# A two-block transformer kernel: the merged attention in another order over its units, and two splits moved

## What is computed

```python
# layer 0, eight heads each, four blocks of 128 queries, causal
logits = einsum(q, k) * 96**-0.5;  p = softmax(where(k_idx <= q_idx, logits, -1e30));  o1 = p @ v
z = einsum(q, k) * 64**-0.5                          # stick breaking
mask = k_idx < q_idx
log_1m_beta = where(mask, log_sigmoid(-z), 0)
suffix = cumsum(log_1m_beta, reverse) - log_1m_beta
o2 = where(mask, exp(log_sigmoid(z) + suffix), 0) @ v
# mixer of the second block
qk = silu(causal_depthwise_conv(xn @ w_in[:, :2048], conv_w, conv_b))      # width 4
# each expert, on its block of 128 rows
hb = silu(xb @ w1[e]) * (xb @ w3[e]);  out = hb @ w2[e]
```

## Time and profile before

| | |
|---|---|
| median of 3 runs (lowest to highest) | 2888.7 us (2888.36 to 2888.79) |
| the profiled execution | 2887.3 us |
| its span, first to last instruction | 2885.6 us |
| mean granted TensorE clock | 0.939 |
| merged attention | about 142 to 320 us |
| mixer's projection | about 1448 to 1604 us |
| expert loop | about 2240 to 2830 us |

### The profile page before, as it was taken

The page is one execution under the profiler, slowest core; times in us unless marked ns, Lnnn a source line. Parts: engine busy times, 40 slices in busy tenths (PEclk is TensorE's granted clock), DMA queues, the critical chain, the costliest instruction groups (busy, mean ns, idle before and its releaser), DMA issues. The chain is left out here.

```text
span 2885.6 us, 30599 instructions
## 1 busy us (share of the span) xinstructions
PE 2657.8 (92%) x12110; PEld 2158.0 (75%) x12110; DVE 1522.2 (53%) x2085; ACT 1234.1 (43%) x1570; POOL 122.6 (4%) x166
## 2 busy tenths in 40 slices
PE   6998999999998999999989969798995899999994
PEld 5866778888887777888877658677874777877774
DVE  4555444344323654434466443245346788888884
ACT  3366432223334742213222222324242677777773
POOL 0111000000140000000000000000002000000001
PEclk9967799999998999999989989899997899999997
DMA  3300132433431023342322022221304899999993
GB/s 130 119 1 1 50 120 93 139 109 119 138 110 37 1 76 116 108 146 88 117 88 88 30 95 88 73 88 59 142 14 190 345 392 396 395 396 396 396 392 119
DMA packets 157146, 432.84 MB, mean 150 GB/s; under 512 B 11051, under 2 KB 80838, under 8 KB 144582
## 3 DMA queue, kind: packets, MB, share of 16 engines
q1 hardware_dynamic: 148950, 400.90, 38.1%
q10 hardware_dynamic: 4608, 16.78, 1.4%
q0 software_dynamic: 3440, 13.11, 1.3%
HBM read 383.58 MB, written 47.19 MB: 149 GB/s over the span
## 5 line engine op out<-in xcount | busy, mean ns | idle before, releaser
L307 PE MATMUL ps<-area,area 128*128 128x512 f32 (+1 forms) x1696 | 658.5, 388 | 0.0
L330 DVE TENSOR_TENSOR area<-area,area 128x2048 fp32r<-128x2048 f32 (+4 forms) x161 | 340.5, 2117 | 598.5 <-ACT area L324 598.5
L306 PE MATMUL ps<-area,area 128*128 128x512 f32 (+5 forms) x1432 | 552.0, 385 | 0.0
L324 ACT ACTIVATE area<-area 128x2048 fp32r<-128x2048 f32 (+4 forms) x161 | 284.1, 1767 | 615.6 <-PE ps L307 582.4
L2324 DVE TENSOR_TENSOR area<-area,area 128x2048 fp32r<-128x2048 f32 x192 | 433.9, 2286 | 107.3 <-ACT area L2319 107.3
L305 PE MATMUL ps<-actT_parts,area 128*128 128x512 f32 x968 | 385.4, 398 | 11.6 <-DVE area L330 9.4
L306 PE MATMUL ps<-actT_parts,area 128*128 128x512 f32 x968 | 383.3, 396 | 0.0
L2319 ACT ACTIVATE area<-area 128x2048 fp32r<-128x2048 f32 x192 | 361.0, 1913 | 48.5 <-PE ps L2353 18.4
L307 PEld LDWEIGHTS ps<-area,area 128*128 128x128 f32 x1696 | 320.4, 189 | 68.3
L306 PEld LDWEIGHTS ps<-area,area 128*128 128x128 f32 x1432 | 277.5, 194 | 52.8
L305 PE MATMUL ps<-area,actT_parts 128*128 128x512 f32 (+3 forms) x704 | 274.6, 390 | 39.6 <-DVE area L330 30.8
(11 more groups left out here) (329 smaller groups left out, 3205.3 us busy)
## 6 DMA issues: line engine op xcount, KB each, us to landing
area<-in_w SPq DMA_DIRECT2D x96, 2048.0 KB, 10.1
area<-in_w_in SPq DMA_DIRECT2D x16, 2048.0 KB, 7.9
area<-in_l_w_gate SPq DMA_DIRECT2D x22, 1024.0 KB, 5.4
area<-in_l_w_up SPq DMA_DIRECT2D x22, 1024.0 KB, 8.0
expert_inputs<-maskz SPq DMA_DIRECT2D x39, 512.0 KB, 8.7
area<-in_l_w_in SPq DMA_DIRECT2D x9, 2048.0 KB, 8.2
area<-expert_inputs SPq DMA_DIRECT2D x32, 512.0 KB, 9.7
expert_rows<-area ACTq DMA_DIRECT2D x32, 512.0 KB, 8.6
```

Source lines behind the costliest of these rows:

```text
L306: pe.matmul(dst(r), a.l, b.h, start=False, stop=False)
L307: m = pe.matmul(dst(r), a.h, b.l, start=False, stop=end)
L324: eng.activation(w.h, raw, ACT.Copy).then_inc(w_hi, 1)
L330: dve.tensor_tensor(w.l, raw, w.high_f, ALU.subtract).then_inc(w_lo, 1)
```

## The change

```diff
-                            score_banks=(0, 1), turn_banks=(2,), value_banks=(6,), prep_bank=2)
+                            score_banks=(0,), turn_banks=(2,), value_banks=(6,), prep_bank=2)
...
             def sb_bank(v):
-                return ps[:, 3 + v % 2, 0:causal(v)]
+                return ps[:, (1, 3, 4)[v % 3], 0:causal(v)]
...
             def two_pe(pe, ch):
-                for v in range(U0 + 4):
-                    sb_pe(pe, v)
-                    mla.pe(pe, v)
+                for v in range(U0 + 5):
+                    sb_scores(pe, v)
+                    mla.pe_preps(pe, v)
+                    mla.pe_scores(pe, v)
+                    sb_turn(pe, v - 4)
+                    mla.pe_values(pe, v - 3)
+                    mla.pe_turn(pe, v - 2, v)
+                    sb_values(pe, v - 5)
 
             def two_act(act, ch):
                 act.preload_act_table_set("natural_log_exp_and_others")
-                for v in range(U0 + 3):
-                    sb_act(act, ch, v)
-                    mla.act(act, v)
+                for v in range(U0 + 4):
+                    mla.act_copy(act, v - 3)
+                    if v:
+                        mla.act_exp(act, v - 1)
+                    t1 = T1[:, v % 4, 0:causal(v)]
+                    if v < U0:
+                        act.wait_ge(b_sc, v + 1)
+                        if v >= 4:
+                            act.wait_ge(b_w, v - 3)
+                        ch.mark(act.activation(t1, sb_bank(v), ACT.Abs))
+                    taken = ch.n
+                    mla.act_preps(act, v)
+                    if v < U0:
+                        ch.wait(taken)
+                        ch(act.activation(t1, t1, ACT.Exp, scale=-1.0))
+                        act.activation(t1, t1, ACT.Ln, bias=1.0).then_inc(b_t1, 1)
+                    sb_weights(act, v - 3)
+                    sb_copy(act, v - 4)
 
             def two_dve(dve, ch):
-                for v in range(U0 + 5):
-                    sb_dve(dve, ch, v)
-                    mla.dve(dve, ch, v)
+                for v in range(U0 + 6):
+                    sb_logs(dve, v - 1)
+                    mla.dve_out(dve, ch, v - 4)
+                    sb_out(dve, v - 6)
+                    sb_scan(dve, ch, v - 1)
+                    sb_less(dve, ch, v - 1, ch.n)
+                    mla.dve(dve, ch, v)
```

**Mixer's projection**, on ScalarE and on VectorE alike:

```diff
-                    if c % 4 == 3:
+                    if c % 4 == 1:
                         msp.after(act, at_qk[j])
```

**Experts**, on VectorE:

```diff
                         if q == p:
                             gated(dve, n)
-                        if q == p + 2:
+                        if q == p + 1:
                             turned_low(dve, n)
```

More of the change, by code:

```diff
@@ L870, in pe, with pe_preps @@
             def pe(self, pe, v):
-                units, nsc, npt = self.units, len(self.sc_banks), len(self.pt_banks)
+                self.pe_preps(pe, v)
+                self.pe_scores(pe, v)
+                self.pe_turn(pe, v - 2, v)
+                self.pe_values(pe, v - 3)
+            def pe_preps(self, pe, v):
                 for n, (at, _, blocks, _, _) in enumerate(self.preps):
@@ L880, in pe, with pe_scores @@
                         m.then_inc(s_pr, 1)
-                if self.mlstm and v < units and v % NT == 0:
+            def pe_scores(self, pe, v):
+                nsc = len(self.sc_banks)
+                if self.mlstm and v < self.units and v % NT == 0:
                     if v:
@@ L884, in pe @@
                     self.exponents(pe, v // NT).then_inc(s_pr, 1)
-                if v < units:
+                if v < self.units:
                     if v >= nsc:
@@ L888, in pe, with pe_turn @@
                     self.scores(pe, v, self.bank(v), self.pre0).then_inc(s_sc, 1)
[L889 to L890 removed]
+            def pe_turn(self, pe, u, v):
+                npt = len(self.pt_banks)
+                if 0 <= u < self.units:
                     pe.wait_ge(s_ex, self.ex0 + u + 1)
@@ L899, in pe, with pe_values @@
                     m.then_inc(s_pt, 1)
-                if 3 <= v < units + 3:
-                    u = v - 3
+            def pe_values(self, pe, u):
+                if 0 <= u < self.units:
                     pe.wait_ge(s_pe, self.pe0 + u + 1)
@@ L911, in act, with act_preps @@
             def act(self, act, v):
-                units = self.units
+                self.act_preps(act, v)
+                self.act_copy(act, v - 2)
+                self.act_exp(act, v)
+            def act_preps(self, act, v):
                 for n, (at, done, _, d, gain) in enumerate(self.preps):
@@ L925, in act, with act_exp @@
                     act.activation(self.PT[:, u % 2, 0:L], self.turned(u, 0, L), ACT.Copy).then_inc(s_pe, 1)
-                if v < units:
+            def act_exp(self, act, v):
+                if v < self.units:
                     L = self.length(v)
@@ L943, in act, with dve_out @@
                                        accum_out=col(rs, v)).then_inc(s_ex, 1)
[L945 to L949, removed]
+            def dve_out(self, dve, ch, u):
+                if 0 <= u < self.units:
                     h, i = divmod(u, NT)
@@ L954, in dve @@
                     dve.tensor_scalar(self.dst(h, i), self.value_at(u), col(rinv, u), None, ALU.mult).then_inc(s_on, 1)
-                    last = False
+            def dve(self, dve, ch, v):
+                units, mlstm, length = self.units, self.mlstm, self.length
+                last = 4 <= v < units + 4 and len(self.vb) > 1
                 if v < units:
@@ L1470, in sb_pe, with sb_weights @@
                     m.then_inc(b_o, 1)
[L1472 to L1482, removed]
+            def sb_weights(act, u):
+                if 0 <= u < U0:
                     act.wait_ge(b_m2, u + 1)
@@ L1492, in sb_act, with sb_scan, sb_less, sb_logs @@
                     act.activation(PT2[:, u % 2, 0:L], ps[:, 5, 0:L], ACT.Copy).then_inc(b_pe, 1)
-            def sb_dve(dve, ch, v):
-                if 5 <= v < U0 + 5:
-                    u = v - 5
+            def sb_scan(dve, ch, u):
+                if 0 <= u < U0:
+                    L = causal(u)
+                    dve.wait_ge(b_m1, u + 1)
+                    if u >= 4:
+                        dve.wait_ge(b_pt, u - 3)
+                    ch.mark(dve.tensor_tensor_scan(Pb2[:, u % 4, 0:L][:, ::-1], ones[:, 0:1].to_broadcast([P, L]),
+                                                   T1[:, u % 4, 0:L][:, ::-1], 0.0, ALU.mult, ALU.add))
+            def sb_less(dve, ch, u, scanned):
+                if 0 <= u < U0:
+                    p = Pb2[:, u % 4, 0:causal(u)]
+                    ch.wait(scanned)
+                    dve.tensor_tensor(p, sb_bank(u), p, ALU.subtract).then_inc(b_w, 1)
+            def sb_logs(dve, u):
+                if 0 <= u < U0:
+                    dve.wait_ge(b_t1, u + 1)
+                    t1 = T1[:, u % 4, 0:causal(u)]
+                    dve.scalar_tensor_tensor(out=t1, in0=sb_bank(u), scalar=0.0, in1=t1,
+                                             op0=ALU.max, op1=ALU.add).then_inc(b_sp, 1)
+            def sb_out(dve, u):
+                if 0 <= u < U0:
                     h, i = divmod(u, NT)
@@ L1512, in sb_dve, with drop_sums @@
[L1512 to L1516, removed]
+            def drop_sums(po, u):
+                if 0 <= u < U0:
+                    dg = T1[:, u % 4, causal(u) - P:causal(u)]
+                    po.wait_ge(b_sp, u + 1)
+                    po.affine_select(out=dg, in_=dg, compare_op=ALU.is_gt, fill=0.0,
+                                     base=0, pattern=[[-1, P]], channel_multiplier=1).then_inc(b_m1, 1)
@@ L1518, in two_po, with drop_weights @@
+            def drop_weights(po, u):
+                if 0 <= u < U0:
+                    dg = Pb2[:, u % 4, causal(u) - P:causal(u)]
+                    po.wait_ge(b_w, u + 1)
+                    po.affine_select(out=dg, in_=dg, compare_op=ALU.is_gt, fill=NEG,
+                                     base=0, pattern=[[-1, P]], channel_multiplier=1).then_inc(b_m2, 1)
             def two_po(po, ch):
                 for v in range(U0 + 1):
[L1520 to L1530, removed]
-            def two_pe(pe, ch):
-                for v in range(U0 + 4):
-                    sb_pe(pe, v)
-                    mla.pe(pe, v)
+                    drop_sums(po, v)
```

32 lines of the change are left out of this document (11 added, 21 removed).

## The result

The changed kernel takes **2813.6 us** (median of four runs, 2811.63 to 2813.82) against 2888.5 for the kernel before, a ratio of 0.9742 with a 95% interval of 0.9728 to 0.9756. The forecast was 2833, faster, with a range of 2808 to 2874: the side and the range held, and 75 us were gained where 56 were forecast. The profiled execution took 2813.81 us with a span of 2812.0.

What follows compares the result with a forecast made beforehand. A loop through ScalarE, VectorE and TensorE was taken to set the merged attention's pace, with TensorE's work inflated by the low clock. Merged attention -33, mixer -9, experts -14: 2887.3 - 56 + 1.4 = 2832.7 us, range 2808 to 2874.

Steps and rivals of the forecast that it cites:

- point (a): Merged attention: VectorE's logarithm step belongs to the unit before, so the value product waits for a logarithm finished an iteration ago.
- point (c): Merged attention: the stick-breaking score comes first in TensorE's iteration, so ScalarE's three activations run during five other TensorE steps.
- The low clock of the second head: Merged attention: one head at the low clock, 25.0 us, and 5 us given back for one more clock drop.
- The later heads: Merged attention: six heads at the high clock, 14.8 us each, 88.8 us together.
- The drain: End of the merged attention: 9 us for the last units, against 14 before.
- The bound of -49: Merged attention: best case, seven heads at the high clock, 103.6 us, plus 9 us of drain.
- The single bank: Merged attention: one softmax score bank makes a loop of some 3.1 us, hidden under 3.45; one wait, some 0.9 us a head.
- (b): Merged attention: the transposes come a unit later, so their exponentials are done and TensorE need not wait.
- Rival 4: Expert loop: the edit does nothing because the transfers bind; -42 in all, 2847 us; chance 0.12.
- The first, the clock up at once: Merged attention: sustained activity releases the throttle from the first full head; -72 in all, 2817 us; chance 0.14.
- The second: Merged attention: the single softmax bank binds, 0.6 us more a unit; -40 in all, 2849 us; chance 0.16.
- The third: Merged attention: the clock stays low, 25.0 us a head, stage 28 us longer; +5 in all, 2894 us; chance 0.08.

Runs made afterwards that it cites:

- the filling: The changed kernel with idle identity transposes in the first units' stops, 12 more ahead of unit 4's softmax score than in the shorter filling: 2803.7 us.
- the shorter filling: The changed kernel with 32 idle identity transposes: 8 and 6 behind the first two preparations, 6 ahead of the softmax score in units 1 to 3: 2810.9 us.

## Why the prediction was right, and where it was short

**What bounds it.** Right in the main. The loop over L1515, L954 and L907 costs what the prediction says, through its waits and through the clock: with the logarithm put back the stage took 231.6 us. That it would come out slower than the old kernel had not been foreseen. Which share of the 48.7 us the lag of the logarithm, point (a), brings alone, and which the early score, point (c), was not tested.

**Merged attention, -33 forecast, -48.7 measured.** The mechanism held, three sizes were off.

- *The low clock of the second head* ("one head at the low clock (25.0) ... I give back 5 for one more drop of the clock"). The head took 19.0 us, as the clock rose in its midst at 172 us: 6 us. The clock did not fall again: 5 us.
- *The later heads*, 14.0 us and not 14.8: 4 us over five heads. The 13.8 for TensorE's work at the high clock was too much: it is busy for 13.2 us a head (65.82 over five), so the low clock's 25.0 should have been divided by 1.9 and not by 1.81. The wait of 0.76 us stands where 0.9 was put.
- *The drain*, 0.7 us.

Together 15.7. The bound of -49 has the measured value by luck: it puts the second head at 14.8 instead of 19.0, 4.2 us too few, and the five later ones 4 us too many. The reason for the give-back was that I had read the low stretch from 282 to 302 as a sign that dense work can stay low. It can, but here no dense head fell back once the clock was high.

**The single bank.** Hidden as forecast, but for one wait a head (0.76 us; two banks saved 0.8). The sign "ScalarE's idle time is the smallest" did not come: over five heads TensorE is busy 65.8 us of 70.0, ScalarE 65.0.

**The third stick-breaking bank buys no wait.** Right.

**The transposes a unit later** (b) were named as one of three things that leave TensorE's path. Wrong for this version: undone, nothing was lost. With two softmax banks the lag is worth 0.6 us a head (13.8 with the filling and without the lag, 13.2 without the filling and with it).

**Mixer, -9 forecast, -9.5 measured.** Right in both terms that it names: the stop from 8.41 to 1.46 and the clock kept behind it. That the sum fits so well is partly luck: the wait of 1.01 us that went at a later split had been put at nothing, and the longer second stretch at 0.50 took back 1.7 us. The lower bound's mechanism (a later piece becomes late) did not come. One unit further ahead something became late, but it was the next filter and not a piece.

**Experts, -14 forecast, -16.9 measured.** The 0.56 us an expert held (18.62 to 18.07). The 3 us deducted for transfers were not needed: 407 GB/s at landing times of 9.9 us. Rival 4 falls.

**The rivals.** The first, the clock up at once, with -72 and 2817, is nearer to the measured 2813.6 than the forecast's 2833. Its mechanism came late: the first 14 of the second head's 19 us were still at 0.50. The page it rests on (the Trainium skill, "TensorE: Matmul & The Clock Gate", Part 1) says that sustained activity releases the throttle; here the release came at 172 us, 14 us into the second head, and held to the end of the stage. The second and the fourth are excluded by the runs with two banks each and with the experts' edit alone. The third did not happen; but the kernel with the logarithm step back shows that its mechanism exists, a stage at 0.52 with 28.3 us a head.

## What to carry to other kernels

When several engines in order share a loop, look for the step that makes one engine wait for work of the same iteration on another, and give it one iteration of lag: here that step was worth 103 us of a 232 us stage within the new order, the other lag nothing. Price such a loop at both levels of the clock, since short waits also lower the clock and most of the loss was there (12 of 14.3 us a head), and look at the start of the stage: 44 idle transposes in the first stops brought 8 us. Moving work ahead pays until what it delays comes late, and one step too far cost 36 us in the expert loop and 7 in the mixer.

## What the runs showed of the hardware that was not expected

- The same dense stretch of matmuls, the last head without preparations, ran wholly at 0.50 before (19.82 busy us of 20) and wholly at 1.00 after. It is not bound to the level at which it begins: in the kernel before with the experts' edit alone, the same order of instructions began this head at 0.50 at 283.8, rose at 292.7 in its midst and was back at 0.50 at 299.5.
- With the shorter filling two stops of TensorE close together, 1.33 and 0.78 us, came before a fall of the clock at 158.5, which cost about 5 us in the head behind it (19.1 against 14.6 us). With idle transposes in place of the first stop the second did not bring the clock down. So a stop far shorter than the 8.41 us of the mixer can matter, and transposes of the identity are enough to prevent it.
- The clock also fell without any stop: in the mixer's projection of the changed kernel, at 1445.2, while TensorE worked through the 8-column products of the gates (14.00 busy us of the 14 before).
- A DMA share of 1.00 did not mean that the queues were full: 396 GB/s became 407 with landing times a little shorter (10.3 to 9.9 us).
